# Three row tiles per operand behind three norms, and the values of a head pair in one group

## What is computed

```python
n = rmsnorm(h, g_mix); z = n @ w_in                      # q, k, v | u | gates
q = partial_rotary(q, positions); k = partial_rotary(k, positions)
# dilated attention and state space, gated, @ w_out; ffn; ple; then rmsnorm(h, g_final)
h = rmsnorm_2(x, norm1_g[l]) * (1.0 + scale1) + shift1
proj = h @ w_in[l]                                       # x_rnn, q_lat, kv_lat, k_rope, g_rnn, g_mla
xc = causal_dwconv(x_rnn, conv_w[l], conv_b[l]); y_rnn = rg_lru(xc, ...)
y_mla = causal_block_attention(q, k, v)                  # softmax over causal blocks, 16 heads
x = x + gate1 * (merged @ w_out[l])
h2 = rmsnorm_2(x, norm2_g[l]) * (1.0 + scale2) + shift2
u = causal_dwconv(h2 @ w_up[l], ffn_conv_w[l], ffn_conv_b[l])
x = x + gate2 * ((jax.nn.silu(u_gate) * u_val) @ w_down[l])
```

## Time and profile before

| | us |
|---|---|
| median of 3 runs | 1797.94 |
| lowest and highest | 1797.42, 1798.92 |
| the profiled execution | 1797.43 |
| its span, first to last instruction | 1795.6 |
| TensorE busy in it | 1778.1 |
| VectorE, ScalarE, GpSimd busy | 1042.5, 786.9, 268.2 |

### The profile page before, as it was taken

How to read it: one execution, slowest core, us unless ns; L and a number is a source line. 1 busy time by engine, 2 the same in 40 slices (tenths; PEclk the granted TensorE clock), 3 DMA queues, 4 the chain that set the end, 5 groups by cost and what they waited for, 6 DMA issues and landing times.

```text
span 1795.6 us, 20963 instructions
## 1 busy us (share of the span) xinstructions
PE 1778.1 (99%) x8086; PEld 1416.3 (79%) x8086; DVE 1042.5 (58%) x1675; ACT 786.9 (44%) x1248; POOL 268.2 (15%) x349
## 2 busy tenths in 40 slices
PE   9999999999999999999999999999999999999998
PEld 7888888878887888888887678766668778888887
DVE  8864554756566544554478796256545675435543
ACT  6554554524344221222264666356643454224443
POOL 4776536300000000000001110322210000000000
PEclk9999999999999999999999999999999999999999
DMA  6222223134344545554341322411143233333332
GB/s 216 95 88 89 71 89 92 51 115 151 94 147 164 188 141 180 207 188 152 118 135 59 130 93 78 140 65 59 36 142 111 78 104 94 94 94 94 94 94 71
DMA packets 65411, 202.06 MB, mean 113 GB/s; under 512 B 7520, under 2 KB 11872, under 8 KB 65312
## 3 DMA queue, kind: packets, MB, share of 16 engines
q1 hardware_dynamic: 65312, 200.72, 34.2%
HBM read 192.30 MB, written 8.40 MB: 112 GB/s over the span
## 4 chain that ended last, share of the span: by engine, by line
PE 93%; DVE 3%; ACT 2%; issue 1%; DMA 0%; SPq 0%; POOL 0%; ACTq 0%; DVEq 0%; POOLq 0%
PE bank L258 28%; PE bank L260 28%; PE bank L259 28%; PE bank L659 2%; PE bank L687 1%; PE bank L672 1%; PE bank L304 1%; DVE wlo L1454 1%; PE bank L356 1%; PE bank L341 1%; PE bank L537 1%; ACT whi L856 0%; PE bank L386 0%; PE bank L377 0%; PE bank L300 0%
## 5 line engine op out<-in xcount | busy, mean ns | idle before, releaser
L258 PE MATMUL bank<-tiler,whi 128*128 128x512 f32 x2260 | 911.9, 403 | 6.0 <-DVE wlo L1454 2.8
L260 PE MATMUL bank<-tiler,wlo 128*128 128x512 f32 x2260 | 892.0, 395 | 0.0
L259 PE MATMUL bank<-tiler,whi 128*128 128x512 f32 x2260 | 891.7, 395 | 0.0
L856 ACT ACTIVATE whi<-raw 128x1024 fp32r<-128x1024 f32 x284 | 298.8, 1054 | 512.2 <-PE bank L260 504.1
L258 PEld LDWEIGHTS bank<-tiler,whi 128*128 128x128 f32 x2260 | 425.7, 188 | 120.4 <-issue 16.6
L260 PEld LDWEIGHTS bank<-tiler,wlo 128*128 128x128 f32 x2260 | 425.1, 188 | 100.6
L259 PEld LDWEIGHTS bank<-tiler,whi 128*128 128x128 f32 x2260 | 425.6, 188 | 97.7 <-issue 1.7
L1454 DVE TENSOR_TENSOR wlo<-raw,whi 128x1024 fp32r<-128x1024 f32 x263 | 326.7, 1246 | 264.2 <-ACT whi L856 263.9
L2279 POOL TENSOR_TENSOR stat<-stat,scl 128x4 f32<-128x4 f32 x7 | 7.5, 1079 | 751.4 <-DVE stat L1962 429.7
L2270 POOL TENSOR_TENSOR wlo<-raw,whi 128x1024 fp32r<-128x1024 f32 x21 | 49.9, 2376 | 212.6 <-ACT whi L856 212.6
L2218 DVE SCALAR_TENSOR_TENSOR tile<-bank,sm,tile 128x511 f32<-128x511 f32 x42 | 31.5, 750 | 85.8 <-ACT tile L1418 54.1
(11 more groups left out here) (381 smaller groups left out, 1578.2 us busy)
## 6 DMA issues: line engine op xcount, KB each, us to landing
raw<-wst SPq DMA_DIRECT2D x284, 512.0 KB, 3.7
wide<-wadaT SPq DMA_DIRECT2D x52, 512.0 KB, 3.5
tile<-xT SPq DMA_DIRECT2D x16, 256.0 KB, 6.1
spare<-tile SPq DMA_DIRECT2D x16, 256.0 KB, 2.1
tile<-spare SPq DMA_DIRECT2D x16, 256.0 KB, 6.0
out<-tile SPq DMA_DIRECT2D x8, 256.0 KB, 2.5
tile<-gblk SPq DMA_DIRECT2D x5, 256.0 KB, 4.5
us<-tile SPq DMA_DIRECT2D x4, 256.0 KB, 2.0
```

Source lines behind the costliest of these rows:

```text
L258: e.matmul(bank, whi[:, o:o + 128], hi, start=start, stop=False)
L259: e.matmul(bank, whi[:, o:o + 128], lo, start=False, stop=False)
L260: e.matmul(bank, wlo[:, o:o + 128], hi, start=False, stop=stop).then_inc(*sig("blk", n))
L856: e.activation(whi[:, c % NHL * W:(c % NHL + 1) * W], raw[:, c % NRAW * W:(c % NRAW + 1) * W], ACT.Copy).then_inc(*sig("hi", c))
```

## The change

Behind the norms n1, nn and n3 TensorE interleaves three row tiles with each operand instead of two (`proj3`): tiles 0, 12 and 24 of `in`, 2, 3 and 4 of `in2`, 1, 23 and 2 of `up`. Tile 24 goes to bank 4 instead of 6. The order of the weights in HBM follows. On ScalarE the copies of the raw tiles, which free banks for the third tile, stand between the high halves: the first right behind k = 0. The requests for chunks have other places: at nn and n3 one chunk ahead of the operands, the next behind k = 3 on ScalarE (ahead of the scaling of k = 4 on VectorE), the next behind k = 6 (ahead of k = 7), and one right behind the operands. The gate groups, the maxima and one exponential of the recurrent layer come one tile later; SyncE's loads stand two tiles further ahead of its stores at nn. In latent attention all four `mtimes` of an odd head stand in a row, behind `mturn(h, 3)` and the last `side` blocks.

```diff
+        def up_at(m, x):
+            return first.get(("up", 0), 0) + 16 * m + 8 * x if m in (1, 2) else first.get(("up", m + 22 * x), 0)
...
+            def proj3(a, b, c, ops, need, freed_by=None):
+                for k in range(len(ops)):
+                    proj(*a, ops, [k], 0, need)
+                    proj(*b, ops, [k])
+                    if freed_by and k == 0:
+                        e.wait_ge(*at(*freed_by))
+                    proj(*c, ops, [k])
...
-                    if a == 0 and part < 2:
+                    if a == 0:
                         if part == 0:
-                            proj2("in", 0, B[0], "in", 12, B[1], N1, "n1")
+                            proj3(("in", 0, B[0]), ("in", 12, B[1]), ("in", 24, B[4]), N1, "n1", ("u_raw", 0))
                         continue
-                    if s == 2:
-                        e.wait_ge(*at("u_raw", 2))
-                    else:
-                        e.wait_ge(*free_a(s - 2))
-                    bank = B[6 if s == 2 else s % 2]
+                    e.wait_ge(*free_a(s - 2))
+                    bank = B[s % 2]
...
-            proj2("in2", 2, ba, "in2", 3, bb, NN, "nn")
+            proj3(("in2", 2, ba), ("in2", 3, bb), ("in2", 4, bank("conv", 4)), NN, "nn")
             spread("r1", 30, B[7])
-            for m in range(4, 24):
+            for m in range(5, 24):
...
-                if m < 14:
-                    gate_rnn(m - 4)
+                if m < 15:
+                    gate_rnn(m - 5)
...
                     side(h, 5)
-                    if h % 2:
-                        mtimes(h, 0)
-                        mtimes(h, 1)
                     mturn(h, 3)
                     side(h, 6)
                     side(h, 7)
                     if h % 2:
-                        mtimes(h, 2)
-                        mtimes(h, 3)
+                        for kb in range(4):
+                            mtimes(h, kb)
...
-                    ba, bb = bank2(p, "cv_g", m), bank2(p + 1, "cv_u", m)
+                    if m == 1:
+                        proj3(("up", 1, bank2(2, "cv_g", 1)), ("up", 23, bank2(3, "cv_u", 1)), ("up", 2, bank2(4, "cv_g", 2)), N1, "n3")
+                    elif m == 2:
+                        proj("up", 24, bank2(5, "cv_u", 2), N1)
+                    else:
+                        proj("up", m, bank2(p, "cv_g", m), N1)
+                        proj("up", 22 + m, bank2(p + 1, "cv_u", m), N1)
...
-                        if k in (1, 3, 4, 6):
-                            u_raw((0, 0, None, 1, 2, None, 3)[k])
+                        if k in (0, 3, 4, 6):
+                            u_raw((0, None, None, 1, 2, None, 3)[k])
...
             halves("n1", 8, (62, 63, 65), N1)
+            prep(5 * CB)
...
             prep(first.get(("in2", 0), 0))
             sums(7)
+            prep(first.get(("in2", 0), 0) + 8)
             for k in range(8):
...
-                if k in (1, 7):
-                    prep(first.get(("in2", 0), 0) + 8 * (k // 4 + 1))
-            for i in range(2):
-                e.wait_ge(*made("in2", i))
-                e.activation(F(48 + i), B[i], ACT.Copy).then_inc(*sig("raw", i))
-            prep(first.get(("in2", 0), 0) + 24)
+                if k in (0, 2):
+                    e.wait_ge(*made("in2", k // 2))
+                    e.activation(F(48 + k // 2), B[k // 2], ACT.Copy).then_inc(*sig("raw", k // 2))
+                if k in (3, 6):
+                    prep(first.get(("in2", 0), 0) + 8 * (k // 3 + 1))
+            prep(first.get(("in2", 0), 0) + 32)
...
             def modulated(name, rb, w, ops, so, sh, ahead):
                 for k in range(9):
-                    if k == 3:
-                        prep(ahead)
+                    if k in (4, 7):
+                        prep(ahead + (0 if k == 4 else 8))
...
-                prep(ahead + 8)
...
             diagonal("r12", ST_R12, 48)
+            prep(first.get(("in2", 0), 0) + 8)
             e.wait_ge(*at("rb", "r12"))
-            modulated("nn", B[6], SILU, NN, S_GF, 0, first.get(("in2", 0), 0) + 8)
+            modulated("nn", B[6], SILU, NN, S_GF, 0, first.get(("in2", 0), 0) + 16)
...
-            prep(first.get(("in2", 0), 0) + 24)
+            prep(first.get(("in2", 0), 0) + 32)
...
             for k in range(8):
-                until("in2", 3 + k)
+                until("in2", 5 + k)
```

More of the change, by code:

```diff
@@ L1023, in scalar @@
                 if a < 12:
-                    start_of("in", 24 + m0)
+                    prep(first.get(("in", 24 + m0), 0) if a else 6 * CB)
                     e.wait_ge(*made("in", 12 + m0))
@@ L1224, in scalar @@
                 if m == 15:
-                    for i in range(5, 10):
+                    for i in range(5, 9):
                         lru_exp(i)
                 if m == 16:
+                    lru_exp(9)
                     for i in range(5):
@@ L1397, in scalar @@
                     if m:
-                        prep(first.get(("up", m), 0) + (8 if m < 4 else 0))
+                        prep(up_at(m, 0) + (8 if m < 4 else 0))
                     if m % 11:
@@ L2512, in load_u @@
                         *sig("u4", j, r, by=16))
-            until("in", 24)
+            chunks(12)
             for j in range(4):
```

43 lines of the change are left out of this document (20 added, 23 removed).

## The result

The changed kernel takes 1801.38 us (median of 9 runs, 1799.71 to 1802.81), the kernel before 1796.82 on the same chip (9 runs, 1795.89 to 1798.92). The ratio is 1.0025, with a 95% interval of 1.0017 to 1.0033: 4.6 us slower (3.1 to 5.9). The profiled execution has a span of 1800.7 us at a granted clock of 0.998. The forecast was 1798.3, with a range up to 1800.8.

What follows compares the result with a forecast made beforehand. TensorE, busy 99% of the span, bounds the kernel, so only its few gaps can be won. Terms +1.0 + 0.3 + 0.45 - 1.4 = +0.35 gave a forecast median of 1798.3 us, range 1793.5 to 1800.8.

Steps and rivals of the forecast that it cites:

- stage 1: Stretch behind norm n1, matmuls from 33.39: operands gain 1.7 us, later waits outweigh it, net +1.0 us.
- wait for the key copy: Ahead of s = 3, TensorE waits 2.1 us for ScalarE's copy of key tile 0 out of bank 1; +0.5 us.
- rotation, first scores: VectorE's first rotation, 4.20 us long, ends at 58.3; TensorE's first scores come at 57.9 and wait until 58.4.
- stage 2: Stretch behind norm nn, from 953.04: the 1.9 us wait goes, but tile 6 waits for bank 2; +0.3 us.
- values of a pair: Odd heads' value matmuls in one group for 7 of 8 pairs, saving 0.20 us each: -1.4 us.
- stage 3: Stretch behind norm n3, from 1423.69: TensorE waits for bank 2, then a chunk, until 1452.95; +0.45 us.
- The rule of the Trainium skill on rotating banks: Groups should rotate through banks so evacuation overlaps matmuls; by it stage 1 pays, stages 2 and 3 don't.
- the diagonal of r1: In stage 2, VectorE finishes it at 969.7, just in time for TensorE at 970.0.
- Rival 1: Operands do gain in stages 2 and 3: -5.8 us, 1792.1 us; chance 0.15 in full or nearly, 0.04 halfway.
- The restart: TensorE's cost after a value group, to be paid in either order; counting it too gave the bound -2.3 us.
- Rival 2: Stage 1's lag repeats in 12 attention steps, 0.35 us each: 4.2 us more, 1802.5 us; chance 0.07.

Runs made afterwards that it cites:

- u_after_rotation: The changed kernel with GpSimd's four U scalings waiting for VectorE's first rotation: 1798.13 us against 1797.08 for the kernel before, +1.05 us.
- stage1_old_late: The changed kernel with stage 1 as before and VectorE's chunks one operand later in nn and n3: 1791.27 us against 1797.08 for the kernel before, -5.8 us.
- values_alone: The kernel before with only the values of a head pair merged into one group: 1795.40 us against 1797.42, -2.0 us.
- stage1_alone: The kernel before with only the edits of stage 1 (three row tiles per operand behind n1): 1802.69 us against 1797.17, +5.5 us.
- after_again: The changed kernel unaltered, timed and profiled once more: 1801.19 us against 1797.17 for the kernel before, +4.0 us.
- stages23_alone: The kernel before with stages 2 and 3 in the new form, stage 1 and values as before: 1798.91 us against 1797.17, +1.7 us.
- u_later: The changed kernel with GpSimd's four U scalings behind its last powers and VectorE's first rotation: 1799.32 us against 1797.42 for the kernel before, +1.9 us.
- late_requests: The changed kernel with VectorE taking each chunk of nn and n3 one operand later: 1796.70 us against 1797.42 for the kernel before, -0.7 us.
- stage1_repaired: The changed kernel with later chunk requests, U scalings behind the rotation, chunk 8 copied earlier, sine and cosine first: 1792.42 us against 1797.08 before, -4.7 us.
- stage1_undone: The changed kernel with stage 1 as before (two row tiles per operand): 1795.31 us against 1797.42 for the kernel before, -2.1 us.
- before_u_early: The kernel before with GpSimd's four U scalings ahead of its powers, beside VectorE's first rotation: 1797.82 us against 1797.08, +0.7 us.

## Why the prediction was wrong

It named the places and missed one price. Its terms, against what the trace of the changed kernel and the runs show:

| step | forecast | measured |
|---|---|---|
| 24 blocks of stage 1 without a gap, wait for the key copy | 2.1 wait, +0.5 | 2.0 wait, +0.5 |
| rotation, first scores | 0.5 wait, stage 1 **+1.0** | 3.5 wait and half clock, stage 1 **+5.7** |
| stage 2 | +0.3 | +1.2 |
| values of a pair | -1.4 | -2.2 |
| stage 3 | +0.45 | +0.9 |
| sum | +0.35 | +5.6 by the traces (+5.0 with the 0.65 won ahead of stage 1), +4.6 by the medians |

**The failed step** is the one on the earlier trace rows: "its rows run from 51.63 to 55.15 + 0.68 = 55.83, 4.20 us", and then "so it now ends at 58.3". It moved VectorE's chain by 2.5 us and kept its length. But at 55.98 GpSimd begins four scalings of 128x512; the prediction weighed only ScalarE's and VectorE's rows there. Moved later, the chain lies beside the scalings. And these did not even keep their place: they begin at 53.51, 2.5 us earlier, since the five small rows ahead of them no longer have the rotation beside them and take 1.0 us (52.39 to 53.42) instead of 2.9 (53.02 to 55.90). Price: 3.1 us of longer rows, and, because TensorE's wait grew from 0.5 to 3.5, about 1.6 us at half clock behind it. 1.0 + 3.1 + 1.6 = 5.7, as measured. With the scalings out of the way (u_after_rotation) the rows, the wait and the clock up to the first scores are those of the forecast, and TensorE is 4.6 us less late there.

The Trainium skill says this of the two engines (SBUF — State Buffer, Who interferes with whom): a VectorE instruction with two inputs in SBUF contends with a GpSimd instruction that reads SBUF, and so does a scaling or copy in its fast two-port mode, while an instruction with one input and outside that mode does not; it speaks of an exclusive lock for the whole instruction. The trace agrees on the kinds of rows: those of tensor with tensor and the scaling (0.49 alone, 1.54 beside GpSimd's scalings) are longer, the shuffle (0.73 alone, 0.75 beside them) is not. Held against the rows of GpSimd, this rule would have shown the place. It would not have given the size: in the kernel before the same two engines also worked side by side, and VectorE's rows took 4.20, against 4.01 with GpSimd idle.

The rule of the Trainium skill on rotating banks (Perfetto Trace Analysis, Matmuls), which the prediction weighed, told the sign of stage 1 and, as the sum did, not its size.

**Stages 2 and 3** went as forecast in their mechanism: VectorE's idle times in stage 2 were 1.26, 1.08 and 1.08 (forecast 1.36, 1.2, 1.2), the diagonal of r1 was in time, and the waits came where they were expected. Up to 1065 stage 2 cost nothing (forecast +0.3). The prediction said of the gate groups, maxima and exponentials that they "keep their distance to each other, so I count nothing for them"; this missed a wait of 0.8 for the diagonal of nk at 1071, 1.2 with what follows it. VectorE's chunk ahead of that diagonal starts 6.4 later than before (1050.35, now 1056.79), one row of maxima (L2006, 0.69) has come to stand behind it, and the diagonal starts 7.05 later (1063.70, now 1070.75), where TensorE is 5.0 later. In stage 3 the forecast missed the 0.4 ahead of the first block. Rival 1 was wrong about the kernel as changed, but right about what limits it: with the requests one operand later most of its gain comes.

**Values of a pair**: the group now stands in the trace as one row, answering to the earlier trace rows:

```profile
1233.08 2.37 PE L695 MATMUL bank<-tile 128*64 128x512 f32 x16
1235.39 0.50 PE L261 MATMUL bank<-tiler,whi 128*128 128x512 f32 x1
```

The mechanism was right, the size at the bound that the prediction gave (-2.3): 0.31 per group saved. The restart, 0.1 us, which I took to be paid in either order, goes too.

**Rival 2** (a lag that repeats in the attention loop) did not occur: from the first scores to the beginning of stage 2 the lag grew by 0.1 in 890 us. In eight of the 14 traces, which run the same rows there, it shrinks by 1.5 instead; what that is stands in the last section.

## What to carry to other kernels

When an edit moves a chain of one engine, lay it over the rows of every engine that shares something with it at the new time, not only over those it waits for: a chain that ended 0.15 us ahead of GpSimd's large rows lay beside them when it was moved by 2 us (and they themselves came 2.5 us earlier), and moving those rows in turn laid them beside the next ones. A wait of TensorE has two prices, its length and the slower clock that may follow. In these traces that began at 2.2 us from start to start, so a wait that grows to that length is to be costed with a surcharge of up to 1.6 us. And a difference of 1.5 us between two medians can come from a stretch that the edit never touches, so the trace has to show where it arose. And where an operand feeds more matmuls, the requests that stand between the operands set the pace: moving two of them by one operand turned stages 2 and 3 from a loss of 1.7 us into a gain of 3.8 (stage1_old_late less values_alone).

## What the runs showed of the hardware

**How often the clock falls behind a wait.** In the 14 traces I took every idle time of TensorE behind the start of stage 1, measured from start to start of its matmuls, and looked at the pace of the matmuls behind it (0.232 us, or 0.427 at half clock). Of 22 between 1.15 and 1.55 us, and of 13 between 1.85 and 2.11, none was followed by the slow pace; of 22 between 2.2 and 2.35, seven were; of the three between 3.3 and 3.9, all. Each time some eight matmuls were slow, 1.6 us in all. The same wait of 2.3 us ahead of s = 3 was followed by it in stage1_alone, in slices of 2 us:

```profile
50.00:52.00 2.00, 0.42 (x2) 0.38 (x3) 1.23 (x1) 1.95 (x4) 1.84 (x4) 1.00 0.00 0
52.00:54.00 2.00, 2.00 (x8) 1.64 (x7) 0.43 (x1) 2.00 (x4) 1.84 (x7) 0.72 0.04 8
54.00:56.00 2.00, 2.00 (x6) 1.52 (x5) 1.92 (x4) 0.90 (x2) 2.00 (x2) 0.50 0.18 71
```

but not in the changed kernel. In stage1_alone it fell at a place where VectorE's rotation hid it: the wait ahead of the first scores was 1.9 in place of 3.5. The kernel before has two such waits as well (stages 2 and 3); in its trace the clock held behind both, in that of values_alone it fell behind both. That may be part of why the executions of one kernel spread over 2 to 7 us; it was not tested by itself. What decides between falling and holding at 2.3 us stays open.

**Two paces at full clock.** In the stretch from 570 to 940 of the trace before (1587 matmuls, none of them waiting, granted clock 1.00) the same matmuls take 370.07 us from first to last in six traces (before, after, after_again, stage1_alone, stages23_alone, u_later) and 368.56 in the other eight, each to 0.01 us. In the stretch from 1465 to 1780 (1357 matmuls) they take 315.11 us in eleven, and 316.40 in late_requests, stage1_old_late and stage1_repaired. So one and the same wait-free stretch has two lengths, 1.5 and 1.3 us apart. The kernel before and the changed kernel have the same pace in both stretches, so their comparison is not touched. That of either with stage1_undone, values_alone, before_u_early or u_after_rotation is, at least by the profiled executions. What sets the pace stays open, and whether a kernel keeps one in all its executions wasn't seen: only the changed kernel was profiled twice (the same both times).

**Who pays in a collision.** It depends on the rows. Beside GpSimd's four rows of 128x512 VectorE's rotation went from 4.20 to 7.30 us, and GpSimd's four from 5.97 to 6.09 (6.84 in before_u_early); no trace has those four without any VectorE row beside them. Beside GpSimd's small rows it was the other way round: a row of 128x16 took 0.66 us instead of 0.21 in the kernel before and 0.75 in u_later, while the rotation took 4.20 and 4.04, against 4.01 with GpSimd idle (u_after_rotation).
